# Evictions ahead of weights, the input's forms a chunk later, and two plain chunks per up projection, in a two-block decoder kernel

## The reference

```python
# first block
for layer in range(2):
    mix = even_mixer(rmsnorm(h)) if layer == 0 else odd_mixer(rmsnorm(h))   # MLA + dilated attention / sliding window
    h = h + mix
    h = h + (silu(gate) * up) @ w_down            # gate, up = rmsnorm(h) @ w_gate_up, width 2816
h = rmsnorm(h)
# second block
for layer in range(2):
    h = h + (gla_mixer(rmsnorm(h)) if layer == 0 else diff_mixer(rmsnorm(h), shared k, v))
    h = h + square(relu(rmsnorm(h) @ w1)) @ w2    # width 4096
```

## Time and profile before

| | |
|---|---|
| three timed runs | 2316.94, 2317.35, 2317.39 us (median 2317.35) |
| profiled execution | 2313.32 us, span 2311.5 us |
| TensorE (PE) busy | 2226.1 us, 96% of the span, 13274 matmuls |
| weight loads of TensorE (PEld) busy | 1929.6 us, 83% |
| VectorE (DVE) busy | 1663.5 us, 72% |
| ScalarE (ACT) busy | 1133.4 us, 49% |
| mean granted TensorE clock | 0.986 |
| read from HBM | 202.76 MB, 89 GB/s over the span |

### The profile page before, as it was taken

The page is one execution under the profiler, slowest core; times in us unless marked ns, Lnnn a source line. Parts: engine busy times, 40 slices in busy tenths (PEclk is TensorE's granted clock), DMA queues, the critical chain, the costliest instruction groups (busy, mean ns, idle before and its releaser), DMA issues.

```text
span 2311.5 us, 32777 instructions
## 1 busy us (share of the span) xinstructions
PE 2226.1 (96%) x13274; PEld 1929.6 (83%) x13274; DVE 1663.5 (72%) x2488; ACT 1133.4 (49%) x1833; POOL 0.2 (0%) x4
## 2 busy tenths in 40 slices
PE   9999799999999799999999979999999998899999
PEld 7677699999777799998799868998977766798997
DVE  5755878797676878797677786776755776776774
ACT  5654544444473544354535443543545884533442
POOL 0000000000000000000000000000000000000000
PEclk9999999999999899999999989999999999999999
DMA  4221132232222122232311212222232112232322
GB/s 153 87 84 73 55 110 95 98 110 77 97 92 74 73 96 106 101 110 74 115 65 56 92 62 103 103 98 95 88 116 73 55 55 73 74 110 92 110 83 100
DMA packets 37302, 206.96 MB, mean 90 GB/s; under 512 B 4256, under 2 KB 4768, under 8 KB 17824
## 3 DMA queue, kind: packets, MB, share of 16 engines
q1 hardware_dynamic: 34560, 199.17, 24.1%
q10 hardware_dynamic: 2592, 5.70, 0.8%
HBM read 202.76 MB, written 2.10 MB: 89 GB/s over the span
## 4 chain that ended last, share of the span: by engine, by line
PE 84%; DVE 8%; ACT 6%; issue 2%; DMA 1%; SPq 0%; ACTq 0%; DVEq 0%
PE ps L940 31%; PE ps L345 15%; PE ps L347 14%; PE ps L346 14%; PE ps L1431 2%; ACT high_w L393 2%; DVE low_w L414 1%; ACT xh L580 1%; DVE h L871 1%; PE ps L2631 1%; DVE squares_sq L632 1%; PE ps L1486 1%; ACT forms_th L608 1%; PE ps L1455 1%; ACT squares_sq L602 1%
## 5 line engine op out<-in xcount | busy, mean ns | idle before, releaser
L414 DVE TENSOR_TENSOR low_w<-raw_w,high_w 128x2048 fp32r<-128x2048 f32 (+4 forms) x211 | 420.4, 1994 | 114.9 <-ACT high_w L393 114.2
L393 ACT ACTIVATE high_w<-raw_w 128x2048 fp32r<-128x2048 f32 (+4 forms) x211 | 351.9, 1669 | 143.1 <-DMA raw_w<-in_w_m_dn 93.1
L345 PE MATMUL ps<-ffn_hidh,high_w 128*128 128x512 f32 x864 | 336.5, 390 | 0.0
L346 PE MATMUL ps<-ffn_hidl,high_w 128*128 128x512 f32 x864 | 336.3, 389 | 0.0
L347 PE MATMUL ps<-ffn_hidh,low_w 128*128 128x512 f32 x864 | 336.1, 389 | 0.0
L940 PE MATMUL ps<-forms_th,forms_s 128*128 128x256 f32 x864 | 246.3, 285 | 24.4 <-ACT forms_kept L986 12.9
L940 PE MATMUL ps<-xh,high_w 128*128 128x256 f32 x864 | 247.1, 286 | 0.7 <-DVE low_w L414 0.7
L940 PE MATMUL ps<-xl,high_w 128*128 128x256 f32 x864 | 246.4, 285 | 0.0
L940 PE MATMUL ps<-xh,low_w 128*128 128x256 f32 x864 | 246.2, 285 | 0.0
L940 PE MATMUL ps<-forms_th,form_lows_s 128*128 128x256 f32 x864 | 245.9, 285 | 0.0
L940 PE MATMUL ps<-form_lows_t,forms_s 128*128 128x256 f32 x864 | 245.7, 284 | 0.0
(11 more groups left out here) (347 smaller groups left out, 4601.3 us busy)
## 6 DMA issues: line engine op xcount, KB each, us to landing
raw_w<-in_w_f_gu SPq DMA_DIRECT2D x44, 1024.0 KB, 4.8
raw_w<-in_w_m_up SPq DMA_DIRECT2D x32, 1024.0 KB, 4.8
raw_w<-in_w_m_dn SPq DMA_DIRECT2D x24, 1024.0 KB, 4.8
raw_w<-in_w_f_dn SPq DMA_DIRECT2D x8, 1024.0 KB, 4.8
raw_w<-in_w_m_dn SPq DMA_DIRECT2D x16, 512.0 KB, 3.4
raw_w<-in_w_b_qk SPq DMA_DIRECT2D x8, 1024.0 KB, 4.8
raw_w<-in_w_f_dn SPq DMA_DIRECT2D x8, 896.0 KB, 4.6
raw_w<-in_w_f_dn SPq DMA_DIRECT2D x16, 448.0 KB, 3.2
```

Source lines behind the costliest of these rows:

```text
L345: pe.matmul(out, sh, mh, start=start, stop=False)
L346: pe.matmul(out, sh, ml, start=False, stop=False)
L393: act.activation(wh[slot][:, 0:elems], raw[slot][:, 0:elems], ACT.Copy).then_inc(w_rounded, 1)
L414: dve.tensor_tensor(wl[slot][:, 0:elems], raw[slot][:, 0:elems], wh[slot][:, 0:elems].bitcast(F32), ALU.subtract).then_inc(w_split, 1)
```

## The change

- **Scaling.** The two scaled tiles `xf` that the forms start from are made by ScalarE in `forms_high` instead of by VectorE in `forms_dve`; the buffer is free again when the former chunk's forms are made.
- **Order in folded projections, VectorE.** The eviction and the fold come first in each chunk, then `sum_weights(c + 2)` and `split_weights(c + 2)`, then `forms_low(n - 2)` and `forms_dve(n - 1)`. Ahead of the first chunk, weights are split up to `base + 2` where forms are made and up to `base + 1` elsewhere. What is left of the forms follows after the last chunk.
- **Order in folded projections, ScalarE.** The fold comes first, then `round_weights(c + 2)`, then `forms_high(n - 1)`; the last `forms_high` follows after the last chunk.
- **Plain chunks.** The first up projection of each feed-forward part starts with two plain chunks (`PLAIN = 2`), so there are 68 formed chunks in place of 72. The root sums stay behind the first of them; the hidden tiles of the first are finished during the second.

Projections without a fold keep their order.

```diff
--- before.py
+++ after.py
@@ -172,10 +172,11 @@
                 down = stage(same, W[f"w_m_dn{i}"], n * P, KD, layer * KD)
             st_mlp[layer].append((up, down, n))
 
+    PLAIN = 2
     FORM_OF = {}
     for parts in (st_ffn[0], st_ffn[1], st_mlp[0], st_mlp[1]):
         for i, (up, _, _) in enumerate(parts):
-            for n in range(0 if i else 1, up.count):
+            for n in range(0 if i else PLAIN, up.count):
                 FORM_OF[up.base + n] = len(FORM_OF)
 
 
@@ -604,7 +605,13 @@
 
     def forms_high(act, F, n):
 
-        wait_for(act, F.s["formed"], 5 * n + 5)
+        s = F.s
+        if n:
+            wait_for(act, s["formed"], 5 * n)
+        for t in range(2):
+            act.activation(xf[:, t, :], h[:, 2 * n + t, :], ACT.Copy, scale=F.weight(2 * n + t))\
+               .then_inc(s["formed"].sem, 1)
+        wait_for(act, s["formed"], 5 * n + 5)
         act.activation(th[:, n, :, :], traw[:, n, :, :], ACT.Copy).then_inc(F.s["fhigh"].sem, 1)
 
     def fold_dve(dve, F, n):
@@ -635,10 +642,6 @@
 
 
         s = F.s
-        wait_for(dve, F.after.added, n + 1)
-        for t in range(2):
-            dve.tensor_scalar(xf[:, t, :], h[:, 2 * n + t, :], F.weight(2 * n + t), None, ALU.mult)\
-               .then_inc(s["formed"].sem, 1)
         wait_for(dve, s["formed"], 5 * n + 2)
         dve.tensor_tensor(traw[:, n, 0:2, :], xf[:, 0, :].rearrange("p (b c) -> p b c", b=2), xf[:, :, HT:TOK],
                           ALU.subtract).then_inc(s["formed"].sem, 1)
@@ -842,24 +845,30 @@
     def resid_act(act, R):
 
         def one(c, n):
-            round_weights(act, c + 2)
             if R.fold:
                 fold_act(act, R.fold, n)
                 if n == R.st.count - 1 and not R.fold.inner:
                     sums_high(act, R.fold)
-                if R.fold.forms:
-                    forms_high(act, R.fold, n)
+            round_weights(act, c + 2)
+            if n and forms:
+                forms_high(act, R.fold, n - 1)
+
+        forms = R.fold and R.fold.forms
+        if forms:
+            round_weights(act, R.st.base + 2)
         each_chunk(R.st, one)
+        if forms:
+            forms_high(act, R.fold, R.st.count - 1)
 
     def resid_dve(dve, R):
         def one(c, n):
             par = R.pair(c)
-            if c + 2 in FORM_OF:
+            if not R.fold:
                 split_weights(dve, c + 1)
                 sum_weights(dve, c + 2)
                 split_sums(dve, c + 2)
-            else:
-                split_weights(dve, c + 2)
+                if c + 2 not in FORM_OF:
+                    split_weights(dve, c + 2)
             dve.wait_ge(w_used, c + 1)
             to, made = h[:, n * R.nt:(n + 1) * R.nt, :], ps[:, 2 * par:2 * par + R.nt, :]
             if R.rooted:
@@ -873,11 +882,20 @@
                 fold_dve(dve, R.fold, n)
                 if n == R.st.count - 1 and not R.fold.inner:
                     sums_low(dve, R.fold)
-                if R.fold.forms:
-                    forms_dve(dve, R.fold, n)
-                    forms_low(dve, R.fold, n)
+            sum_weights(dve, c + 2)
             split_weights(dve, c + 2)
+            if n and forms:
+                if n > 1:
+                    forms_low(dve, R.fold, n - 2)
+                forms_dve(dve, R.fold, n - 1)
+
+        forms = R.fold and R.fold.forms
+        split_weights(dve, R.st.base + (2 if forms else 1))
         each_chunk(R.st, one)
+        if forms:
+            forms_low(dve, R.fold, R.st.count - 2)
+            forms_dve(dve, R.fold, R.st.count - 1)
+            forms_low(dve, R.fold, R.st.count - 1)
 
 
     class Up:
@@ -886,7 +904,7 @@
 
         def __init__(self, st, fold, swiglu, prev, root, flip):
             self.st, self.fold, self.swiglu, self.prev, self.root = st, fold, swiglu, prev, root
-            self.flip, self.plain = flip, 1 if root else 0
+            self.flip, self.plain = flip, PLAIN if root else 0
             n = st.count * (1 if swiglu else 2)
             self.s = marks(up_sems, dict(scaled=self.plain + (st.count if swiglu else self.plain),
                                          acted=st.count if swiglu else 2 * st.count, made=st.count,
@@ -926,7 +944,8 @@
                     last = mm3(pe, ps[:, 2 * par + j, :], w_h[:, b, at], w_l[:, b, at], xh[:, k, :], xl[:, k, :],
                                k == 0, k == KD - 1)
             last.then_inc(w_used, 1)
-            root_pe(pe, U.fold)
+            if n == 0:
+                root_pe(pe, U.fold)
 
         def formed(c, n):
             f, par = FORM_OF[c], U.pair(c)
@@ -1018,7 +1037,15 @@
 
         def one(c, n):
             if n < U.plain:
-                root_act(act, U.fold)
+                if n == 0:
+                    root_act(act, U.fold)
+                elif U.swiglu:
+                    silu(n - 1)
+                    rounded(n - 1)
+                else:
+                    square(n - 1)
+                    rounded(n - 1)
+                    rounded(n - 1, 1)
                 round_weights(act, c + 2)
             elif U.swiglu:
                 if n:
@@ -1079,13 +1106,18 @@
         def plain(c, n):
             par = U.pair(c)
             split_weights(dve, c + 1)
+            if n:
+                made(n - 1)
             sum_weights(dve, c + 2)
+            if n:
+                low(n - 1)
             dve.wait_ge(w_used, c + 1)
             wait_for(dve, *U.fold.root)
             if U.swiglu:
                 dve.tensor_tensor(sq[:, par, :], ps[:, 2 * par, :], rstd[:, :], ALU.mult)\
                    .then_inc(s["scaled"].sem, 1)
             else:
+                wait_past(dve, s["acted"], 2 * n)
                 dve.tensor_copy(sq[:, 0, :], ps[:, 2 * par, :]).then_inc(s["scaled"].sem, 1)
             dve.tensor_copy(xf[:, par, :], ps[:, 2 * par + 1, :]).then_inc(s["scaled"].sem, 1)
 
```

## The result

The changed kernel takes 2256.95 us (median of 4 runs, 2253.22 to 2260.14) against 2317.37 us before (4 runs, 2316.94 to 2318.62): ratio 0.9738, 95% interval 0.9721 to 0.9755, 60.4 us less. The forecast was 2263.6 us, range 2250 to 2284.

A forecast was written before the change was run, and what follows sets the result against it. TensorE, busy 96% of the span, bounds the kernel; waits for late tiles were the target. Terms -50 - 7 + 6 - 2.7 = -53.7 us, off the median 2317.35 (4.0 above the profiled execution): 2263.6 us, range 2250 to 2284.

The forecast's parts named there:

- The schedule of the first passage: Output projection into first up projection: step times from fourth eviction (227.1) onward; TensorE waits 2.2, 0.65 and 3.95 us.
- The four passages: From attention or GLA output projections into first up projections: 12.5 us gained each, 50 us; slow clock costs 6 back.
- The other three projections: Last down projections feeding a norm: gains of 1.9, 2.0 and 3.1, 7 us; another 2.7 from the clock.
- The 0.4 us a chunk: Down projection ahead of GLA: VectorE's round 5.2 us against TensorE's 4.8, so TensorE waits about 0.4 us, six times.
- One slow stretch of 1.5 us a passage: TensorE's clock after the new waits of 2.2 and 4.0 us in each passage: 6 us lost in all.
- rival C: Each of the two new waits brings its own slow stretch: 4 x 1.5 us more, 2270; chance 0.10.
- 2.2 us for the slow clock: First formed chunk of the kernel before: said to lose up to 2.2 us to a slow TensorE clock.
- The scaling at "nothing" on ACT: Scaled tiles on ScalarE, about 1.34 us a pair: costs nothing while ScalarE waits for VectorE; 21 us without that cover.
- B: VectorE's chain grows by 5 us or more, or `forms_kept` queues longer: passages give 6 or 7, near 2287; chance 0.17.
- D: TensorE starves for weights in narrow projections: round of 7.0 us, 2.2 us lost per chunk, slower; chance 0.05.
- E: Better than forecast: no slow clock and a short kept wait, 2252 us; chance 0.04.
- F: Late tiles stay late for a reason the semaphores hide: no change; chance 0.02.

The follow-up runs named there:

- run 1: The changed kernel again without an edit, against the kernel before on the same chip: 2257.12 us, ratio 0.9740.
- run 5: Changed kernel, but the three last down projections feeding attention or GLA have weights ahead of the eviction again, as before: 2266.39 us, ratio 0.9788.
- run 10: Changed kernel with three plain chunks and the scaling of the input's tiles back on VectorE: 2247.14 us, ratio 0.9701.
- run 2: Changed kernel with one plain chunk instead of two; new orders and scaling on ScalarE stay: 2280.36 us, ratio 0.9843.
- run 3: Changed kernel with order, forms and scaling as in the kernel before; only the two plain chunks are left: 2282.21 us, ratio 0.9853.
- run 4: Changed kernel with the scaling of the forms back on VectorE, all else as changed: 2266.12 us, ratio 0.9784.
- run 6: Changed kernel with three plain chunks instead of two: 2231.33 us, ratio 0.9635.
- run 11: The kernel of run 6 again (changed kernel with three plain chunks): 2230.63 us, ratio 0.9631.

## Why the prediction was right

**The schedule of the first passage** came out step by step. Times of after less the 2.53 us of its opening, with the forecast in brackets: fourth eviction 226.9 (227.1), last input remainder done 245.6 (245.85), weight sums done 248.2 (248.4), plain chunk's evictions done 249.4 (249.6), sums' split done 251.1 (251.3), weights' split done 253.3 (253.5). The waits are 2.07, 0.51 and 3.50 us (2.2, 0.65, 3.95), and the down projection starts at 317.7 (316.5, and 1.5 for the clock). The chain consists of operations of DVE and ACT whose durations all stand in the trace of before, which is why adding rows up worked.

**The four passages**: 46.9 us in the first profile and 45.3 in run 1, where -50 and +6 give 44. One by one they are 11.2, 14.2, 11.3 and 10.2 us shorter; the last lies under the 11 to 14 that were forecast. **The other three projections**: 8.8 in the profile, 10.9 in run 1's and 9.3 by run 5, where 7 and 2.7 give 9.7. The 0.4 us a chunk in the down projection ahead of GLA are there: its chunks start 5.2 us apart (1057.94, 1063.18, 1068.41, 1073.61, 1078.83) with 4.8 us of matmuls in each. So are the 1 to 2 us waits for `low_w` (1.91 at 584.50, 1.48 at 1663.46). Behind the one at 584.50 came a slow stretch of 1.6 us, which neither the forecast nor run 1 has.

**The clock.** One slow stretch of 1.5 us a passage was taken; the four passages show 1.6, 1.2, 1.0 and 2.4, some 6.2 us together (the matmuls of these stretches at their pitch, less as many at the full rate's). But only the first and the last, 4.0 us, lengthen the passage. Windows of the first passage behind the wait of 2.07 us and behind that of 3.50, and the same two of the second passage (columns as in run 10):

```profile
253.72:262.55 8.83, 4.82 (x37) 4.42 (x37) 8.76 (x10) 6.43 (x8) 0.00 (x0) 1.00 0.24 99
262.55:269.50 6.95, 6.95 (x45) 6.95 (x46) 6.88 (x9) 3.73 (x6) 0.00 (x0) 0.75 0.00 0
754.56:763.39 8.83, 6.19 (x36) 5.80 (x36) 8.76 (x10) 6.42 (x8) 0.00 (x0) 0.81 0.23 96
763.39:769.00 5.61, 5.61 (x46) 5.61 (x47) 5.54 (x6) 2.39 (x5) 0.00 (x0) 1.00 0.01 3
```

In the first passage the first wait left the clock at full rate and the second didn't. In the second passage it is the other way round, and the way from the first formed product to the kept one takes the same 8.83 us: ScalarE's copy sets its end, so PE's slow matmuls only shorten the wait in front of it:

```profile
763.39 0.39 PE L959 MATMUL ps<-forms_th,forms_s 128*128 128x256 f32 x1 [2.64 <-ACT forms_kept L1005]
```

That passage takes 113.8 us against 115.3 of the first and of both SwiGLU passages of run 1, where the slow stretch lies behind the kept wait. So here a slow stretch is paid for only behind the last wait. That is why rival C fell, and its price is missing even where both waits bring a slow stretch, as in run 5's fourth passage: it takes 75.7 us, 1.5 more than the third passage of run 1 (74.2), where the only one lies ahead of the kept wait. The prediction's 2.2 us for the slow clock in the first formed chunk of before was no such loss: from the first formed product to the kept one the last two passages of before take 8.84 us each, with the slow stretch (1369.60) and without it (1975.99).

**Two plain chunks' share and the scaling** were costed inside one sum, so the prediction had no number for either alone; the chain's theory, written out before runs 2 to 4, gave 2281, 2285 and 5 to 7 us slower, where 2280.4, 2282.2 and 9.0 slower were measured. The scaling at "nothing" on ACT is right: ACT waits 3.79 us for DVE even now.

**The rivals.** B: the wait ahead of the first formed product is 2.1 in each passage, not 5 or more longer; runs 4 and 10 show what its mechanism costs when DVE does get more to do. D: in the projection ahead of GLA a chunk takes 5.2 us, not 7.0. E: the wait for `forms_kept` is a little shorter than the forecast's 3.95 (3.35 on average; 3.2 before), the slow clock stayed. F: the tiles are in time.

**Where the 6.7 us between forecast and median come from.** The sum was off by 0.5 the other way. The rest, 7.2, is the step from span to median: the profiled execution of before lay 4.0 us under its median, and the forecast put those 4.0 back; that of after lies 3.2 above its own median. Run 1's profile lies 0.1 under its median. One execution places a kernel to some 3 us here, and the offset of one kernel's profile should not have been carried to the other. That the sum fits to 0.5 us is luck in part: in the first profile the passages and the other projections together came out 2.0 us better than 53.7, and the opening 2.5 worse. Run 1, with an opening like that of before, has a span 56.3 us shorter, 2.6 more than the sum.

## What to carry to other kernels

When a late engine's queue is reordered, write its chain out from the last event that it must wait for, in measured durations, and see which consumer stands at its end; work that can cover that end (here chunks that need fewer inputs, though each is 0.8 us dearer) should be added until the chain is covered and no further: one, two, three and four plain chunks gave 2280.4, 2257.1, 2231 and 2234.4 us. The prediction had all numbers for it: it listed 7 us of waits left per passage and did not ask what a third chunk would give. An operation belongs on the engine that waits, even where it takes longer there (9.0 us here with two plain chunks, 16.5 with three). To a wait of some us that a change adds, a slow stretch of 1 to 2.5 us may belong; count it only where no other wait stands behind it to take it up.

## What the runs showed of the hardware

The same wait can cost the clock or not. In runs 6 and 11, the same kernel, PE waits 1.89 us for the same tile (`low_w`, the first matmul of layer 1's mixer; its timeline in each). In run 6 it comes back at full rate, 16 matmuls in 3.1 us; in run 11 near the 1.2 GHz level, 11 in 3.6 us (windows, columns as in run 10):

```profile
576.23 0.50 PE L346 MATMUL ps<-xh,high_w 128*128 128x512 f32 x1 [1.89 <-DVE low_w L415]
```

```profile
576.70:579.80 3.10, 3.10 (x16) 2.53 (x15) 2.12 (x4) 1.37 (x3) 0.00 (x0) 1.00 0.10 38
```

```profile
575.49 0.50 PE L346 MATMUL ps<-xh,high_w 128*128 128x512 f32 x1 [1.89 <-DVE low_w L415]
```

```profile
575.90:579.50 3.60, 3.60 (x11) 2.82 (x10) 2.18 (x4) 1.81 (x4) 0.00 (x0) 0.55 0.12 48
```

The stretch from layer 0's last down projection to the next passage takes 160.8 us in the one and 162.5 in the other. The Trainium skill ("TensorE: Matmul & The Clock Gate", What's actually happening) says that the number of slow matmuls at a kernel's start varies between runs of the same kernel. These two runs show the like behind a wait in the middle of one.

Nor does the length of the wait decide alone. Behind the 2.07 us wait ahead of the first formed product the clock is 1.00 in the first profile's first passage and 0.81 in its second (windows above), and in run 5, behind the same wait of the same length, 0.61; behind the longer wait of 3.23 us in the kernel before it is 1.00. Windows of run 5 and of before:

```profile
251.20:255.40 4.20, 4.19 (x21) 3.90 (x22) 4.17 (x4) 2.30 (x3) 0.00 (x0) 0.61 0.47 191
```

```profile
262.64:266.60 3.96, 3.96 (x33) 3.96 (x34) 2.84 (x5) 1.51 (x5) 0.00 (x0) 1.00 0.02 4
```

So the price of a single wait of 2 to 3 us can be told from rows only as nothing or 1 to 2 us; what decides it was not tried.
